# Two layers of a hybrid diffusion backbone: the prologue laid out anew

## What is computed

```
m = silu(c) @ w_mod[l] + b_mod[l]                 # 9 vectors of 1024 per layer and kind of token
h = rmsnorm(x, g0) * (1 + scale) + shift
x = x + 0.5 * gate * rmsnorm((silu(h @ wg) * (h @ wu)) @ wd, g1)
```

```
h = sin(freq * (feats @ w1 + b1)); h = sin(freq * (h @ w2 + b2))
h = (h @ w3).reshape(n, 2, 2, 256) * exp(-t * abs(decay))
k = concat([h[:, 0], 0, h[:0:-1, 1]])             # forward taps, backward taps
y = irfft(rfft(u, 2n) * rfft(k, 2n))[:n] / (2n) + u * bias
```

## Time and profile before

| what | value |
|---|---|
| median of three runs | 1703.1 us |
| profiled execution, own time | 1699.16 us |
| its span | 1697.3 us |
| TensorE busy | 1615.7 us (95%) |
| VectorE busy | 760.5 us (45%) |
| ScalarE busy | 580.0 us (34%) |
| mean granted TensorE clock | 0.989 |

### The profile page before, as it was taken

One profiled execution on the slowest core, in us unless ns is written; L12 is line 12 of the kernel. 1 busy time (PEld: TensorE's weight loads), 2 busy tenths in 40 slices (PEclk: granted clock), 3 DMA queues, 4 the chain that ended last, 5 costly groups with the idle time before them and its releaser, 6 DMA issues.

```text
span 1697.3 us, 19920 instructions
## 1 busy us (share of the span) xinstructions
PE 1615.7 (95%) x7970; PEld 1239.6 (73%) x7970; DVE 760.5 (45%) x1225; ACT 580.0 (34%) x1082; POOL 28.8 (2%) x52
## 2 busy tenths in 40 slices
PE   6789999999987999999999999999998799999998
PEld 2367777788874777777887777778886477777886
DVE  5553333327357553333355333333735755344333
ACT  2242232225326542232244322323532554233222
POOL 0000000000000000000000000000000000000000
PEclk9899999999999999999999999999999999999999
DMA  8625555433730344443344555533373034333332
GB/s 311 270 111 199 199 209 205 144 113 127 271 128 1 138 184 162 174 163 129 130 162 174 202 217 219 200 131 124 130 270 102 0 138 160 124 138 124 104 114 81
DMA packets 80408, 266.46 MB, mean 157 GB/s; under 512 B 10203, under 2 KB 15612, under 8 KB 78908
## 3 DMA queue, kind: packets, MB, share of 16 engines
q1 hardware_dynamic: 75756, 240.50, 38.8%
q0 software_dynamic: 4560, 24.70, 4.1%
HBM read 258.55 MB, written 6.60 MB: 156 GB/s over the span
## 4 chain that ended last, share of the span: by engine, by line
PE 90%; DVE 8%; ACT 1%; issue 1%; DMA 0%; SPq 0%; DVEq 0%; ACTq 0%
PE bank L609 26%; PE bank L610 25%; PE bank L611 25%; PE bank L586 4%; PE bank L649 2%; PE bank L857 1%; DVE w_lo L1212 1%; PE bank L821 1%; PE bank L629 1%; DVE h L1272 1%; DVE sb_s L1447 1%; PE bank L907 1%; DVE h_lo L1279 1%; ACT prob_t L1134 1%; PE bank L779 1%
## 5 line engine op out<-in xcount | busy, mean ns | idle before, releaser
L609 PE MATMUL bank<-w_hi,h_hi 128*128 128x512 f32 (+1 forms) x1200 | 486.5, 405 | 16.8 <-DVE h_lo L1279 13.7
L1212 DVE TENSOR_TENSOR w_lo<-w_raw,w_hi 128x1024 fp32r<-128x1024 f32 (+3 forms) x348 | 365.9, 1099 | 248.0 <-ACT w_hi L959 247.8
L610 PE MATMUL bank<-w_lo,h_hi 128*128 128x512 f32 (+1 forms) x1200 | 473.1, 394 | 0.0
L611 PE MATMUL bank<-w_hi,h_lo 128*128 128x512 f32 (+1 forms) x1200 | 467.7, 390 | 0.0
L959 ACT ACTIVATE w_hi<-w_raw 128x1024 fp32r<-128x1024 f32 (+3 forms) x348 | 312.4, 957 | 207.6 <-PE bank L611 182.2
L609 PEld LDWEIGHTS bank<-w_hi,h_hi 128*128 128x128 f32 x1200 | 226.3, 189 | 106.9 <-issue 50.3
L611 PEld LDWEIGHTS bank<-w_hi,h_lo 128*128 128x128 f32 x1200 | 226.0, 188 | 50.2
L610 PEld LDWEIGHTS bank<-w_lo,h_hi 128*128 128x128 f32 x1200 | 225.9, 188 | 40.5
L1331 DVE TENSOR_TENSOR hm<-bank,sg 128x256 f32<-128x256 f32 x132 | 55.7, 425 | 440.5 <-ACT sg L1052 440.5
L1052 ACT ACTIVATE sg<-bank 128x256 f32<-128x256 f32 x132 | 50.3, 384 | 566.3 <-PE bank L611 566.2
L609 PE MATMUL bank<-w_hi,hid_hi 128*128 128x512 f32 x528 | 208.6, 395 | 0.0
(11 more groups left out here) (211 smaller groups left out, 1112.5 us busy)
## 6 DMA issues: line engine op xcount, KB each, us to landing
w_raw<-w_gu SPq DMA_DIRECT2D x176, 512.0 KB, 6.3
w_m<-w_mod SPq DMA_DIRECT2D x144, 512.0 KB, 4.3
w_raw<-w_dn SPq DMA_DIRECT2D x48, 384.0 KB, 5.1
w_raw<-w_dn SPq DMA_DIRECT2D x48, 320.0 KB, 4.9
w_raw<-w_in SPq DMA_DIRECT2D x28, 512.0 KB, 6.7
w_raw<-w_dn SPq DMA_DIRECT2D x16, 512.0 KB, 5.3
w_raw<-w_out SPq DMA_DIRECT2D x16, 512.0 KB, 5.8
o_bc<-orow POOLq DMA_DIRECT2D x6, 1024.0 KB, 6.8
```

Of the source, the lines that this page charges most:

```text
L609: mm(out, a_hi, b_hi, start=first, stop=False)
L610: mm(out, a_hi, b_lo, start=False, stop=False)
L611: return mm(out, a_lo, b_hi, start=False, stop=last)
L1212: TT(w_lo[:, s, 0:n], w_raw[:, s, 0:n], w_hi[:, 4 * g.hi + j, 0:n], ALU.subtract).then_inc(unit_lo.sem, 1)
```

## The change

The prologue is written in another order on every engine; the loops behind it are as before.

- x is loaded ahead of the modulation weights. TensorE turns it right after the second filter matmul, into six banks (2 to 7); ScalarE copies all six, and does the three squares and roots there. VectorE's three norms come later, behind the last product of layer 1.
- The parameters are loaded by nine POOL DMAs: of `w3` only the 64 partitions that a layer uses, the decays, one row of bias; constants last. The absolute value of the decays is taken on VectorE between the two arguments, and waits for all nine. All six windows are computed between the two sines.
- Taps use two pairs of banks in turn. Layer 1's first taps and product are placed before layer 0's latent spectrum.
- ScalarE copies every spectrum, nine copies a layer. VectorE only corrects the single rows (`fix_ctx`, `fix_lat`). Context and latent parts are stored apart.
- Four tiles of job 1's `w_mod` have a place of their own (`w_m1`) in the space of the second weight group, whose load now waits for them. Rows of both jobs use bank 7.

```diff
+            sp.dma_start(x_fm[:, :, :], x_in).then_inc(x_loaded.sem, 16)
             for kt in range(KT):
                 sp.dma_start(w_m0[:, kt, :], w_mod[0, 0, kt]).then_inc(mod0_landed[kt].sem, 16)
             sp.dma_start(vec[:, :, :], vecs.rearrange("l p v -> p l v")).then_inc(vec_loaded.sem, 16)
             sp.dma_start(bmod[:, :], b_mod).then_inc(vec_loaded.sem, 16)
-            sp.dma_start(x_fm[:, :, :], x_in).then_inc(x_loaded.sem, 16)
-            for kt in range(KT):
+            for kt in range(4):
+                sp.dma_start(w_m1[:, kt, :], w_mod[0, 1, kt]).then_inc(mod0_landed[8 + kt].sem, 16)
...
             load_group(("gu", 0, 0, 0))
+            sp.wait_ge(mod_used.sem, 12)
             load_group(("gu", 0, 0, 1))
-            sp.wait_ge(f_stored.sem, f_stored.at(DEPTH, 0))
+            sp.wait_ge(f_stored_ctx.sem, f_stored_ctx.at(DEPTH, 0))
+            sp.wait_ge(f_stored_lat.sem, f_stored_lat.at(DEPTH, 0))
...
-            pool.dma_start(f_par[:, :, :], fpar.rearrange("l p v -> p l v")).then_inc(f_cst_loaded.sem, 16)
+            for l in range(DEPTH):
+                own = slice(l * FW, (l + 1) * FW)
+                pool.dma_start(f_w3[own, :], fpar[l, own, FP_W3:FP_W3 + 1024]).then_inc(f_cst_loaded.sem, 16)
+                pool.dma_start(f_dec[:, l, :], fpar[l, :, FP_DEC:FP_DEC + 512]).then_inc(f_cst_loaded.sem, 16)
+                pool.dma_start(f_bias[0:1, l, :], fpar[l, 0:1, FP_BIAS:FP_BIAS + 512]).then_inc(f_cst_loaded.sem, 16)
+            pool.dma_start(f_cst[:, 1280:1283], tneg).then_inc(f_cst_loaded.sem, 16)
+            pool.dma_start(f_cst[:, 1024:1280], consts[:, 2048:2304]).then_inc(f_cst_loaded.sem, 16)
             pool.dma_start(f_cst[:, 0:1024], consts[:, 0:1024]).then_inc(f_cst_loaded.sem, 16)
-            pool.dma_start(f_cst[:, 1024:1280], consts[:, 2048:2304]).then_inc(f_cst_loaded.sem, 16)
-            pool.dma_start(f_cst[:, 1280:1283], tneg).then_inc(f_cst_loaded.sem, 16)
             for l in range(DEPTH):
-                pool.wait_ge(spec_ready.sem, spec_ready.at(l, 1))
-                pool.dma_start(spec[l], f_spec[:, :]).then_inc(f_stored.sem, 16)
-                pool.wait_ge(f_stored.sem, f_stored.at(l, 16))
+                pool.wait_ge(f_fixed.sem, f_fixed.at(l, 1))
+                pool.dma_start(spec[l, :, 3072:SPEC], f_spec[:, 3072:SPEC]).then_inc(f_stored_ctx.sem, 16)
+                pool.wait_ge(f_fixed.sem, f_fixed.at(l, 2))
+                pool.dma_start(spec[l, :, 0:3072], f_spec[:, 0:3072]).then_inc(f_stored_lat.sem, 16)
...
-            pe.wait_ge(f_banks_free.sem, f_banks_free.at(DEPTH, 0))
-            job_turn(0, f_rows[:, 0, :])
-            pe.wait_ge(mod_ready.sem, 1)
-            job_turn(1, f_rows[:, 1, :])
-            pe.wait_ge(x_loaded.sem, 16)
             for tt in range(3):
-                if tt:
-                    pe.wait_ge(x_act.sem, tt)
-                    pe.wait_ge(x_dve.sem, tt)
                 for i in range(2):
                     for k in range(4):
-                        last = tr(bank[TURN[i]][:, k * P:(k + 1) * P], x_fm[:, 4 * i + k, tt * P:(tt + 1) * P], ident[:, :])
+                        last = tr(bank[2 + 2 * tt + i][:, k * P:(k + 1) * P], x_fm[:, 4 * i + k, tt * P:(tt + 1) * P],
+                                  ident[:, :])
                     last.then_inc(x_turned.sem, 1)
-            pe.wait_ge(x_act.sem, 3)
-            pe.wait_ge(x_dve.sem, 3)
+            pe.wait_ge(f_sin.sem, 2)
+            pe.wait_ge(f_cst_loaded.sem, 144)
+            fl = f_cst[:, 0:1024].rearrange("p (t f) -> p t f", t=2)
+            fc = f_cst[:, 1024:1280]
+            def filter_taps(l, tt, pair):
+                own = slice(l * FW, (l + 1) * FW)
+                for dr in range(2):
+                    last = mm(bank[pair + dr][:, :], f_h[own, 1, tt * P:(tt + 1) * P],
+                              f_w3[own, dr * 512:(dr + 1) * 512], start=True, stop=True)
+                last.then_inc(f_h3.sem, 1)
+            def spectrum_ctx(l):
+                pe.wait_ge(f_hs.sem, f_hs.at(l, 1))
...
+            def spectrum_lat(l):
+                pe.wait_ge(f_hs.sem, f_hs.at(l, 3))
+                pe.wait_ge(f_copied.sem, f_copied.at(l, 3))
+                pe.wait_ge(f_fixed.sem, f_fixed.at(l, 1))
+                for to, cols, src in ((4, slice(0, P), f_s), (5, slice(2 * P, 3 * P), f_f), (6, slice(256, 257), f_s),
+                                      (0, slice(P, 2 * P), f_s), (1, slice(3 * P, 4 * P), f_f)):
+                    out = bank[to][0:1, :] if to == 6 else bank[to][:, :]
+                    for kt in range(2):
+                        last = mm(out, fl[:, kt, cols], src[:, 1 + kt, :], start=kt == 0, stop=kt == 1)
+                    last.then_inc(f_sp.sem, 1)
+            filter_taps(0, 0, 0)
+            pe.wait_ge(x_act.sem, 6)
+            filter_taps(0, 1, 2)
+            pe.wait_ge(csil_ready.sem, 1)
+            for kt in range(4):
+                rows0(0, kt)
+            spectrum_ctx(0)
+            filter_taps(0, 2, 0)
+            pe.wait_ge(f_hs.sem, f_hs.at(0, 2))
+            filter_taps(1, 0, 2)
+            for kt in range(4, KT):
+                rows0(0, kt)
+            spectrum_lat(0)
+            job_turn(0, START_ROWS)
+            pe.wait_ge(f_copied.sem, f_copied.at(1, 0))
+            pe.wait_ge(f_fixed.sem, f_fixed.at(0, 2))
+            spectrum_ctx(1)
+            filter_taps(1, 1, 0)
+            filter_taps(1, 2, 2)
+            pe.wait_ge(mod_ready.sem, 1)
+            for kt in range(4):
+                rows0(1, kt)
+            spectrum_lat(1)
+            for kt in range(4, KT):
+                rows0(1, kt)
+            job_turn(1, START_ROWS)
+            pe.wait_ge(f_copied.sem, f_copied.at(DEPTH, 0))
+            pe.wait_ge(f_fixed.sem, f_fixed.at(DEPTH, 0))
...
+            act.wait_ge(f_arg.sem, 1)
+            A(f_h[:, 0, :], f_a[:, :], ACT.Sin).then_inc(f_sin.sem, 1)
+            act.wait_ge(dec_done.sem, 1)
+            for l in range(DEPTH):
+                for tt in range(3):
+                    A(f_win[:, l, tt, :], f_dec[:, l, :], ACT.Exp,
+                      scale=f_cst[:, 1280 + tt:1281 + tt]).then_inc(f_win_done.sem, 1)
+            act.wait_ge(f_arg.sem, 2)
+            A(f_h[:, 1, :], f_a[:, :], ACT.Sin).then_inc(f_sin.sem, 1)
+            for tt in range(3):
+                for i in range(2):
+                    act.wait_ge(x_turned.sem, 2 * tt + i + 1)
+                    A(x[:, tt, 512 * i:512 * i + 512], bank[2 + 2 * tt + i][:, :], ACT.Copy).then_inc(x_act.sem, 1)
+            act.wait_ge(const_ready.sem, 4)
+            for tt in range(3):
+                pre_root(0, tt)
+            (la, lb, lc), (ca, cb, cc) = spectra(f_spec)
             for l in range(DEPTH):
                 if l:
-                    act.wait_ge(f_hs.sem, f_hs.at(l, 0))
-                for tt in range(3):
-                    last = A(f_win[:, tt, :], f_par[:, l, FP_DEC:FP_DEC + 512], ACT.Exp,
-                             scale=f_cst[:, 1280 + tt:1281 + tt])
-                last.then_inc(f_win_done.sem, 1)
-                if l:
-                    act.wait_ge(f_stored.sem, f_stored.at(l, 0))
-                (_, lb, _), (_, cb, _) = spectra(f_spec)
-                for b, k, dst in ((1, 2, cb[:, 0]), (5, 5, lb[:, 0]), (6, 6, lb[:, 1])):
+                    act.wait_ge(f_stored_ctx.sem, f_stored_ctx.at(l, 0))
+                for b, k, dst in ((4, 1, ca[:, 0]), (4, 1, cc[:, 0]), (5, 2, cb[:, 0]), (4, 4, la[:, 0]), (4, 4, lc[:, 0]),
+                                  (5, 5, lb[:, 0]), (0, 7, la[:, 1]), (0, 7, lc[:, 1]), (1, 8, lb[:, 1])):
+                    if l and k == 4:
+                        act.wait_ge(f_stored_lat.sem, f_stored_lat.at(l, 0))
                     act.wait_ge(f_sp.sem, f_sp.at(l, k))
                     A(dst.rearrange("p a b -> p (a b)"), bank[b][:, :], ACT.Copy).then_inc(f_copied.sem, 1)
-            act.wait_ge(const_ready.sem, 4)
-            act.wait_ge(mod_used.sem, 16)
-            for tt in range(3):
-                act.wait_ge(x_turned.sem, 2 * tt + 1)
-                A(x[:, tt, 0:512], bank[TURN[0]][:, :], ACT.Copy).then_inc(x_act.sem, 1)
-            pre_root(0, 0)
+            act.wait_ge(mod_used.sem, 8)
             hi_part(("gu", 0, 0, 0))
             affine(0, 0)
...
+                if n == 0:
+                    dve.wait_ge(f_cst_loaded.sem, 144)
+                    dec = f_dec[:, :, :]
+                    STT(out=dec, in0=dec, scalar=-1.0, in1=dec, op0=ALU.mult, op1=ALU.max).then_inc(dec_done.sem, 1)
...
+            def filter_products(l, tt):
+                pair = (0, 2, 0, 2, 0, 2)[3 * l + tt]
+                dve.wait_ge(f_win_done.sem, f_win_done.at(l, tt + 1))
+                dve.wait_ge(f_h3.sem, f_h3.at(l, tt + 1))
+                if l:
+                    dve.wait_ge(f_sp.sem, f_sp.at(l - 1, 8 if tt else 3))
+                done(TT(f_f[:, tt, :], bank[pair][:, :], f_win[:, l, tt, :], ALU.mult))
```

(44 more changed lines are left out.)

126 lines of the change are left out of this document (37 added, 89 removed).

## The result

The change made the kernel slower, by 0.27%. Its median of nine runs is 1708.4 us (1707.3 to 1710.1), beside 1705.4 us for the kernel before (nine runs, 1700.6 to 1706.4): ratio 1.0027, 95% interval 1.0016 to 1.0038. Each of the nine lies above all nine of before. The forecast was 1699.2, the range 1693.5 to 1704. The profiled execution took 1707.4 us, with a span of 1705.6.

What follows compares the result with a forecast made beforehand. TensorE bounds the main part, so only the prologue counts: its steps put the first gate/up product at 85.2 instead of 89.1, 3.9 us off the 1703.1 median, giving 1699.2; range 1693.5 to 1704.

Steps and rivals of the forecast that it cites:

- Parameters: Start of the prologue: 1.7 MB in nine POOL DMAs land at 12.0 us, with bounds of 11 and 19.
- The gate arrives late: Prologue parameters: fixed cost per POOL DMA, last landing at 19; first product 91.7, +2.6, 1705.7 us; chance 0.13.
- under the products: Layer 0: modulation rows of job 0 run on TensorE during VectorE's tap products, adding no time to the path.
- The rival of the half clock: Prologue matmuls: TensorE's low rate holds from 19 to 77 us; first product 114.0, +24.9, 1728 us; chance 0.06.
- Layer 1 and the tail: End of the prologue: layer 1's latent spectra end at 73.5, then rows, coefficients and low parts; first product 85.2.
- the 1.8 allowed: Layer 1's latent spectra: 1.8 us added to 9.4 for a clock falling in TensorE's wait; bounds 0 and 9.4.
- the rival in which nothing falls: Prologue: clock stays up through the wait at 55 to 62, parameters land at 11; 82.5, -6.6, 1696.5 us; chance 0.13.
- The table load: ScalarE between the exponentials and the second sine: the added load costs 1.28 us, with no drain of 1.38 beside it.
- Interleaving hides one product: Layer 1: placing its first product early removes one product, 3.9 us; the rest still waits for layer 0's copies and corrections.
- I had allowed 3.9 for this: Whole kernel: the profiled execution of before, 1699.2, lay 3.9 us under the median of the runs shown, 1703.1.
- my own signs of being wrong: Whole kernel: a first product beyond 89 us, or a main part differing by more than 2 us, makes the prediction wrong.

Runs made afterwards that it cites:

- the second profile: The kernel before, unchanged, profiled once more: 1706.4 us, span 1704.6.

## Why the prediction was wrong

Its steps, with the time at which each ends or starts:

| step | forecast | measured | off |
|---|---|---|---|
| absolute decays start | 12.0 | 18.8 | +6.8 |
| second sine ends | 19.0 | 25.7 | +6.7 |
| first product on VectorE starts | 22.8 | 29.7 | +6.9 |
| third product starts | 31.6 | 41.5 | +9.9 |
| layer 0's latent spectra end | 44.8 | 54.6 | +9.8 |
| norms start | 58.2 | 68.2 | +10.0 |
| layer 1's latent spectra end | 73.5 | 83.9 | +10.4 |
| first gate/up product | 85.2 | 95.2 | +10.0 |

Of the ten microseconds 6.8 are the parameters and 3.1 are layer 0; the forecast was 3.9 us faster, the medians came out 2.9 slower.

*Parameters: the step that failed.* I had divided the DMA engines' 412 GB/s into halves by bytes, and so 1.7 MB were to land by 12.0. The landing went to 18.8. From 7 us on the queues took turns packet by packet, so GpSimd's share in bytes fell when its own packets became small and the tokens' rows of 12 KB came to stand opposite: from 8 to 12 us it was 64% before (1.07 of 1.67 MB) and 30% in the changed kernel (0.42 of 1.39). The half that I had read from before was an average over its whole load. One stretch the turns do not explain: from 5 to 6 us GpSimd's queue moved 24 packets beside 229, from 6 to 7 none beside 31, together 0.05 MB. What held it there no run shows. The run without SyncE's competing weights took 4.4 us off, the run without the tokens in front 2.2. The two were not run together, so that they add up to the 6.8 is not shown. My rival "The gate arrives late" had the place and the moment (19), for another reason: it put the price on each DMA, and with the same nine DMAs the landing came at 14.4 once SyncE waited. Its 1705.7 came closest to the measured 1708.4.

*Layer 0: a term that I had put at nothing, and the low rate.* Between the first and the third product lie 11.9 us and not 8.8. I had the first modulation rows "under the products" and let the context spectra start as the first product ended. But in TensorE's order the rows stand between the second taps and these spectra. The chain shows it: taps to 32.97, rows for 3.57 us, spectra from 36.54, 2.9 us behind the end of the first product. I had also charged the low rate to the taps alone. The granted clock was 0.50 through 20 to 36 us, so the rows took 3.64 us (1.93 at full rate); the context spectra behind them took 3.0 us, nearly the forecast 2.8. With TensorE kept busy 9.4 us lie between the two products, so 2.5 of the 3.1 are the clock. The rival of the half clock was wrong in its extent (in layer 0 it is over by 37 us), right in its mechanism.

In the kernel before the clock's row says 1.00 for 15 to 20 us, while four tap records take 3.76 us as at the low rate. That I took the rate there from the lengths of the records was right: in the changed kernel, at 0.50, eight took 7.19.

*Layer 1 and the tail: right.* From the third product to the first gate/up product the forecast had 53.6 us and 53.7 were measured; its pieces are off by up to 0.4 either way, so that the sum fits to 0.1 is luck. TensorE's wait was 6.9 us (7.3 forecast), released by the correction of the context bin; the clock behind it fell to 0.54 and 0.61, and the spectra took 12.0 (11.2 with the 1.8 allowed; against the 9.1 of layer 0 the clock cost 2.9). So the rival in which nothing falls is out. The table load costs its 1.28 us. The Trainium skill (ScalarE: Activation LUTs, What ACT_TABLE_LOAD costs) has a drain of 1.38 us beside it; in the changed kernel the exponentials end at 23.88, the load starts at 23.91 and the sine at 25.20, so no row shows one. Interleaving hides one product, as said.

*The main part, and the median.* The sum went from one execution of before whose span was 1697.3; its first product at 89.10 came again in the second profile (89.12), its main part of 1608.2 did not (1615.5). The two profiled executions differ by 8.3 us, 6.1 in the prologue and 2.2 behind it. The medians differ by only 2.9, since the median of before lies 6.3 above the execution I started from and that of the changed kernel 1.0 above its own. I had allowed 3.9 for this, from three runs. Both of my own signs of being wrong came: a first product beyond 89, and a main part off by more than 2 us. In the ten profiles with the new prologue and no matmuls added in the mixers the main part lies between 1610.4 and 1612.8. Why the clock behind the same waits differs from execution to execution is open.

## What to carry to other kernels

A wait put on an engine in the middle of its queue costs whatever stands behind it, so place it after the last thing that doesn't need it, and let each consumer wait for its own load instead of all of them. When loads run on two queues, count the packets opposite each other, not the bytes: here 2.75 MB and 1.71 MB on one queue landed at the same time, with the other's large packets taking every second turn. And before a forecast of a few microseconds, profile the kernel before twice: a clock that falls behind short waits can move the base by more than the change.
